# Layers 0 and 1: the first six projection chunks as split products, the narrow columns in two jobs, and buffers moved to equal places modulo 512 bytes

## What is computed

```
h = rmsnorm(x, mix_norm_g)
u = h @ w_in                       # 1024 wide in; columns for four mixers and four gates
y_ret, y_ssd, y_gla, y_ml = mixers(u)
merged = sum_b sigmoid(gate_b) * (y_b @ w_branch_b)
x = x + merged @ w_out
x = x + ffn(rmsnorm(x, ffn_norm_g))      # layer 0: dense; layer 1: experts, top 2 of 8
```

## Time and profile before

| | us |
|---|---|
| median of three executions | 2686.12 |
| the profiled execution | 2694.53 |
| its span | 2692.7 |
| TensorE busy (MATMUL) | 2500.5 (93%) |
| VectorE busy | 1636.8 (61%) |
| ScalarE busy | 1320.3 (49%) |
| GpSimd busy | 407.1 (15%) |
| head of layer 0, chunks 0 to 5 | 27.78 to 115.95 |
| head of layer 1, chunks 0 to 5 | 563.57 to 648.85 |

### The profile page before, as it was taken

One profiled execution on the slowest core, in us unless ns is written; L12 is line 12 of the kernel. 1 busy time (PEld: TensorE's weight loads), 2 busy tenths in 40 slices (PEclk: granted clock), 3 DMA queues, 4 the chain that ended last, 5 costly groups with the idle time before them and its releaser, 6 DMA issues.

```text
span 2692.7 us, 30881 instructions
## 1 busy us (share of the span) xinstructions
PE 2500.5 (93%) x11365; PEld 1986.7 (74%) x11365; DVE 1636.8 (61%) x2327; ACT 1320.3 (49%) x1687; POOL 407.1 (15%) x224
## 2 busy tenths in 40 slices
PE   6999899989998799999999999989998997998998
PEld 5876588878865687777777877868767885776786
DVE  1465655534565598898888988963446544244554
ACT  1343244413332387777777877834534442543443
POOL 2254100003551000000000000024520002551000
PEclk9999899999998899999999999999999998999999
DMA  6433275424241599999999999953456533346550
GB/s 196 142 110 138 99 248 185 139 91 163 94 167 64 173 368 318 322 348 307 322 349 306 331 340 315 343 156 116 151 190 224 188 119 111 135 169 217 188 188 32
DMA packets 373374, 549.30 MB, mean 204 GB/s; under 512 B 20948, under 2 KB 273224, under 8 KB 373144
## 3 DMA queue, kind: packets, MB, share of 16 engines
q1 hardware_dynamic: 369072, 535.82, 58.4%
q0 software_dynamic: 3776, 9.80, 1.3%
q10 hardware_dynamic: 432, 2.37, 0.2%
HBM read 546.91 MB, written 1.05 MB: 203 GB/s over the span
## 4 chain that ended last, share of the span: by engine, by line
PE 65%; DVE 7%; issue 2%; ACT 2%; DMA 2%; POOL 1%; DVEq 0%; SPq 0%; ACTq 0%
PE mb L863 12%; PE mb L865 12%; PE mb L864 12%; PE pb L863 5%; PE pb L865 5%; PE pb L864 5%; PE pb L841 3%; PE pb L1236 2%; PE pb L846 2%; DMA ring<-in_w_in 1%; DVE w_lo L2360 1%; POOL w_lo L719 1%; PE mb L1191 1%; PE pb L932 1%; DVE gates L1911 1%
## 5 line engine op out<-in xcount | busy, mean ns | idle before, releaser
L2360 DVE TENSOR_TENSOR w_lo<-ring,w_hi 128x1024 fp32r<-128x1024 f32 x384 | 461.6, 1223 | 177.8 <-ACT w_hi L1520 128.1
L863 PE MATMUL mb<-w_hi,hT_hi 128*128 128x512 f32 x1232 | 499.0, 405 | 10.6 <-DVE w_lo L2360 6.4
L865 PE MATMUL mb<-w_lo,hT_hi 128*128 128x512 f32 x1232 | 485.1, 394 | 0.0
L719 POOL TENSOR_TENSOR w_lo<-ring,w_hi 128x1024 fp32r<-128x1024 f32 x152 | 370.9, 2464 | 533.3 <-ACT w_hi L1520 533.0
L1520 ACT ACTIVATE w_hi<-ring 128x1024 fp32r<-128x1024 f32 x280 | 285.9, 1054 | 312.2 <-DMA ring<-in_w_in 186.8
L2360 DVE TENSOR_TENSOR w_lo<-down_w,w_hi 128x1024 fp32r<-128x1024 f32 x242 | 295.4, 1223 | 93.3 <-ACT w_hi L1520 79.1
L863 PE MATMUL pb<-w_hi,hT_hi 128*128 128x512 f32 x736 | 300.2, 408 | 10.3 <-DVE low_rows L2360 7.6
L865 PE MATMUL pb<-w_lo,hT_hi 128*128 128x512 f32 x736 | 291.7, 396 | 0.0
L864 PE MATMUL pb<-w_hi,low_rows 128*128 128x512 f32 x736 | 290.9, 395 | 0.0
L1653 ACT ACTIVATE w_hi<-ring 128x1024 fp32r<-128x1024 f32 x256 | 268.1, 1056 | 24.3 <-PE mb L865 18.6
L863 PEld LDWEIGHTS mb<-w_hi,hT_hi 128*128 128x128 f32 x1232 | 232.6, 189 | 62.2 <-DVE w_lo L2360 12.1
(11 more groups left out here) (441 smaller groups left out, 3774.9 us busy)
## 6 DMA issues: line engine op xcount, KB each, us to landing
ring<-in_moe_w SPq DMA_DIRECT2D x128, 1024.0 KB, 7.9
ring<-in_w_in SPq DMA_DIRECT2D x48, 2048.0 KB, 7.9
down_w<-in_moe_w SPq DMA_DIRECT2D x88, 1024.0 KB, 10.6
third_gu<-in_moe_w SPq DMA_DIRECT2D x48, 1024.0 KB, 8.9
down_w<-in_w_ffn_down SPq DMA_DIRECT2D x22, 1024.0 KB, 9.9
ring<-in_w_out SPq DMA_DIRECT2D x8, 2048.0 KB, 8.0
ring<-in_ffn_w SPq DMA_DIRECT2D x16, 1024.0 KB, 8.1
ring<-in_w_ffn_gate SPq DMA_DIRECT2D x16, 1024.0 KB, 5.4
```

What stands on the lines that cost most here:

```text
L719: nc.gpsimd.tensor_tensor(w_lo[:, m % NPIECE], source[m][0], w_hi[:, m % NPIECE].bitcast(F32), ALU.subtract).then_inc(pool_split, 1)
L863: mm(o, a_hi, hi, start=start, stop=False)
L865: return mm(o, a_hi, lo, start=False, stop=stop)
L2360: return tt(dst, src, hi.bitcast(F32), ALU.subtract)
```

## The change

- Chunks 0 to 5 of layers 0 and 1 become split products. `GA` leaves chunk 2, the eight `MI`/`MF` columns leave chunk 4 and the four `SDT` columns leave chunk 5. They have 512 columns each (chunk 4: 256), that is 22 pieces per layer (`HEAD_PIECES`), each with 24 split matmuls of 256 columns. Chunk 2 is loaded by two DMAs of 256 columns.
- The narrow columns are loaded by three small DMAs behind chunk 0, straight to a part of `scratch`, and done as plain fp32 matmuls in two jobs of their own between chunk 0 and chunk 1. The matmuls with `alpha_w` move from behind chunk 5 to behind chunk 1.
- ScalarE rounds the pieces of the head, VectorE takes their low parts. Four pieces are rounded before `hT` is emptied; the high and low parts of `hT` are made bank by bank ahead of chunk 0. VectorE's convolutions are cut into pairs of blocks with low parts between them, and `softplus` is cut in two and moved forward, to the time of chunks 3 and 4. ScalarE's `high_to` calls are spread over the head.
- SP may load a slot again when the low part of its last piece is made.
- ScalarE empties both tokens' halves of a bank with one instruction where before there were two jobs.
- Buffers whose size is an odd multiple of 32 bytes get 32 bytes behind them (`in_lines`), `ea` moves into `small`, and 448 bytes stand between `down_w` and `fhT_hi`.

```diff
+STEP, LINE = 8, 16
 CHUNKS1 = [
-    (SZ, 512, [("ch", ((SX, 128), (SX + 128, 128))), ("tok", 0, SZ, 256), ("tok", 1, SZ, 256)]),
...
-    (SDT, 516, [("ch", ((GQ, 128), (GK, 128))), ("tok2", 0), ("tok2", 1)]),
+    ((SZ, 512), [("toks", SZ, 0), ("ch", SX, 256)]),
+    ((SB, 512), [("ch", SB, 0), ("ch", SC, 256)]),
+    ((GR, 256, MQ, 256), [("toks", GR, 0), ("ch", MQ, 256)]),
+    ((MK, 512), [("ch", MK, 0), ("toks", MV, 256)]),
+    ((MO, 256), [("toks", MO, 0)]),
+    ((GQ, 512), [("ch", GQ, 0), ("toks", GV, 256)]),
...
+NARROW = ((GA, RANK), (SDT, 4), (MI, 8))
...
+        def in_lines(stack, name, shape, dt):
+
+            tensor = stack.enter_context(nc.sbuf_tensor(name, shape, dt))
+            if -(-math.prod(shape[1:]) // STEP) * STEP % LINE:
+                stack.enter_context(nc.sbuf_tensor(name + "_rest", [P, STEP], F32))
+            return tensor
...
+        narrow_w = scratch[:, 256:256 + KD * 28].rearrange("p (k n) -> p k n", k=KD)
-        ea = sb("ea", [P, 2, 4])
+        ea = small[:, 150:158].rearrange("p (l h) -> p l h", l=2)
...
         down_w = sb("down_w", [P, NSLOT, DN_W])
+        sb("down_rest", [P, 112])
...
+                if item[0] == "narrow":
+                    L, at = item[1], 0
+                    if L:
+                        sp.wait_ge(y_ready, 4 * L)
+                    for col, n in NARROW:
+                        sp.dma_start(narrow_w[:, :, at:at + n], a["w_in"][L][:, col:col + n].rearrange("(k p) n -> p k n", p=P)).then_inc(narrow_in, 16)
+                        at += n
+                    continue
...
             def chunk(L, c):
-                lo, n, js = CHUNKS1[c]
-                w = weights((L, "proj", c))
-                for j, spec in enumerate(js):
-                    proj_job(BK[L], ("proj", c, j), w, lo, n, spec)
+                for q in range(count):
+                    m = PC.of[(L, "proj", c, q)]
...
+                    if c == 0:
+                        pe.wait_ge(hT_mix_split, 4 * L + q + 1)
+                    pe.wait_ge(*low_done(m))
...
+                                if kind == "toks":
+                                    it = slice(half * P, (half + 1) * P)
+                                    ins = split_product(bank[:, half * MW:(half + 1) * MW], hT_hi[:, k, it], hT_lo(k)[:, it], m,
+                                                        slice(at, at + MW), first, last)
+                                else:
...
+                                    mm(o, hi, hT_hi[:, k], start=first, stop=False)
+                                    mm(o, lo, hT_hi[:, k], start=False, stop=False)
+                                    ins = mm(o, hi, hT_lo(k), start=False, stop=last)
...
@@ VectorE, mixers(L)
-                acted(B, ("proj", 0, 0))
+                low_range(M0, M0 + 2)
+                hT_low(L, (0, 1))
+                low_range(M0 + 2, M0 + 3)
+                hT_low(L, (2,))
+                low_range(M0 + 3, M0 + 4)
+                hT_low(L, (3,))
...
+                low_range(M0 + 4, M0 + 10)
                 acted(B, ("proj", 1, 1))
...
-                convolve(L, 0, 6, 0, 24)
-                acted(B, ("proj", 3, 0))
-                convolve(L, 6, 4, 30, 46)
-                hT_low(L)
-                acted(B, ("proj", 5, 2))
+                convolve(L, 0, 6, 0, 24, (0, 1))
+                low_range(M0 + 10, M0 + 11)
+                convolve(L, 0, 6, 0, 24, (2, 3))
+                low_range(M0 + 11, M0 + 12)
+                convolve(L, 0, 6, 0, 24, (4, 5))
+                low_range(M0 + 12, M0 + 14)
+                acted(B, ("narrow",))
                 v.wait_ge(alpha_mm, L + 1)
                 softplus(L)
+                low_range(M0 + 14, M0 + 16)
+                softplus_end(L)
+                low_range(M0 + 16, M0 + 19)
+                acted(B, ("proj", 3, 0))
+                convolve(L, 6, 4, 30, 46, (0, 1))
+                low_range(M0 + 19, M0 + 20)
+                convolve(L, 6, 4, 30, 46, (2, 3))
+                low_range(M0 + 20, M0 + 22)
...
@@ ScalarE, before and in mixers(L)
-                turned(BK[L], 0)
+                high_to(MIX[L] + 4)
+                for q in range(4):
+                    turned(BK[L], 0, hT, (q,))
+                    hT_high(L, (q,))
...
+                high_to(M0 + 7)
+                proj(L, 0)
...
+                high_to(M0 + 11)
+                proj(L, 1)
+                high_to(M0 + 15)
+                proj(L, 2)
```

More of the change, by code:

```diff
@@ L10 @@
+import math
 import numpy as np
@@ L167, in bank_jobs1 @@
     jobs = [("turn", k) for k in range(4)]
-    for c, (_, _, js) in enumerate(CHUNKS1):
+    for c, (_, js) in enumerate(CHUNKS1):
         jobs += [("proj", c, j) for j in range(len(js))]
+        if c == 0:
+            jobs += [("ga",), ("narrow",)]
     gate = lambda b, h: [("gate", b, h, i) for i in range(T)]
@@ L196, in split_items1 @@
 def split_items1():
-    items = [("proj", 6), ("proj", 7)]
+    items = [("proj", c) for c in range(len(CHUNKS1))]
     items += [("gate", b, h) for b in range(NBR) for h in range(2)]
@@ L539, in split_item @@
             s = ring_slot()
[L540 to L543 removed]
+            cols = lo if isinstance(lo, tuple) else (lo, 512)
+            width = sum(cols[1::2])
+            count = width * KD // PIECE
+            first = PC.of[(L,) + key + (0,)]
+            loads = []
+            for n, c0 in enumerate(cols[0::2]):
+                at = sum(cols[1:2 * n:2])
+                loads.append((cols_view(width, at), w[:, c0:c0 + cols[2 * n + 1]].rearrange("(k p) n -> p k n", p=P)))
+            add_item((L,) + key, s, loads, low_done(first + count - 1))
+            for q in range(count):
+                source[first + q] = (ring[:, s, q * PIECE:(q + 1) * PIECE], find[(L,) + key] if q == 0 else None)
         def ffn_items(u, L, w1, w3, w2):
@@ new lines, in narrow @@
+            def narrow(L):
+                pe.wait_ge(narrow_in, 48 * (L + 1))
+                for q in range(4):
+                    pe.wait_ge(act_emptied, BK[L].emptied(("turn", q))[1])
+                bank = open_bank(BK[L], ("ga",))
+                for k in range(KD):
+                    ins = mm(bank[0:RANK, 0:S], narrow_w[:, k, 0:RANK], hT[:, k, :], start=k == 0, stop=k == KD - 1)
+                ins.then_inc(filled, 1)
+                bank = open_bank(BK[L], ("narrow",))
+                for i in range(T):
+                    for k in range(KD):
+                        ins = mm(bank[:, 16 * i:16 * i + 12], hT[:, k, i * P:(i + 1) * P], narrow_w[:, k, RANK:], start=k == 0, stop=k == KD - 1)
+                ins.then_inc(filled, 1)
@@ L913, in gate, with alpha @@
+            def alpha(L):
+                acted(BK[L], ("ga",))
+                if L:
+                    pe.wait_ge(gla_put, 5 * L)
+                for i in range(T):
+                    ins = mm(mb[0][:, i * P:(i + 1) * P], ch_in[0:RANK, 12, i * P:(i + 1) * P], alpha_w[:, L, :],
+                             start=True, stop=True)
+                ins.then_inc(alpha_mm, 1)
             def gate(L, b, h, half):
@@ L1395, in _ @@
                     turn(mb[0][:, 0:P], rows, ident).then_inc(rows_turned, 1)
-                for c in range(1, 6):
-                    chunk(L, c)
+                narrow(L)
+                chunk(L, 1)
                 if L == 0:
                     pe.wait_ge(perch_ready, 1)
+                alpha(L)
+                for c in range(2, 6):
+                    chunk(L, c)
                 mixers(L)
@@ L1512, in high_parts, with narrowed @@
+            def narrowed(L):
+                B = BK[L]
+                bank = pb[B.index[("ga",)] % 4]
+                empty(B, ("ga",), (ch_in[0:RANK, 12], bank[0:RANK, 0:S], ACT.Copy, 1.0))
+                both = pb[B.index[("narrow",)] % 4][:, 0:32].rearrange("p (t n) -> p t n", t=T)
+                empty(B, ("narrow",), (u_gla[:, :, 0:4], both[:, :, 0:4], ACT.Copy, 1.0),
+                      (u_ml[:, :, ML_O + MW:], both[:, :, 4:12], ACT.Copy, 1.0))
             def high_parts(lo, hi):
@@ L1875, in norm, with convolve @@
                         op1=ALU.mult).then_inc(xn_ready, 1)
-            def convolve(L, first, count, wcol, bcol):
-                for b in range(count):
+            def convolve(L, first, count, wcol, bcol, blocks):
+                for b in blocks:
                     blk, o = first + b, 50 * L
```

182 lines of the change are left out of this document (94 added, 88 removed).

## The result

| | us |
|---|---|
| before, median of four executions (2684.01 to 2691.84) | 2688.94 |
| after, median of four executions (2663.34 to 2669.47) | 2667.56 |
| ratio, with its 95% interval | 0.9922 (0.9902 to 0.9941) |
| the profiled execution of after | 2668.96 |
| its span | 2667.2 |

The kernel is 21.4 us faster. The forecast was 40 us less, 2646; the time lies in the range of 2630 to 2680. Between the two profiled executions the difference is 25.6 us, because the profiled execution of before was a long one.

The account below looks back on a forecast made before the run. A head lasts as long as its TensorE matmuls. From the profiled 2694.5 us, 16 for the heads and 24 for the buffer places were taken, giving 2654.5; against the median 2686.1 − 40 = 2646, range 2630 to 2680.

Parts of the forecast that it names:

- The price of a product: Heads of layers 0 and 1: a split matmul of 256 columns takes 0.1205 us, between bounds of 0.112 and 0.192.
- The slower rival: Heads: 256 columns don't hide a weight load, 0.192 us a product; 2698 us, without the places' gain 2722; chance 0.09.
- Feeding it: Heads: TensorE waits for VectorE's low parts behind convolutions and softplus, gaps of 10.2 us a layer, a head 81.5 us.
- The starts: Start of chunk 0: layer 1 begins 1.4 us earlier, layer 0 6.0 us later, at 33.8.
- Behind the heads: After the heads: softplus waits (3.8, 3.1 us), slow clock (3.4 a layer) and `xdt` wait (1.1) go; 1.3 a layer lost.
- Heads in all: Layers 0 and 1, heads, starts and what follows: 4.8 and 11.5 us gained, together 16, from 5 to 28.
- The places: Split products of experts and dense down products: realigned operands cut 0.233 to 0.227 us a step, 24 us in all.
- At no cost: Small loads, chunk loads, GpSimd's first piece of chunk 6 and evacuations in layers 0 and 1 stay hidden: 0 us.
- The places not the cause: Dense and expert down products are slow because each goes to another bank, not from buffer places; 2670 us, chance 0.21.
- Experts held by their loads: Experts can't go faster because of their DMA loads, so their 19.5 us are lost; 2665 us, chance 0.07.
- Heads giving nothing: Heads of layers 0 and 1: gaps longer than walked, each brings the clock down; 2662 us, chance 0.07.
- the first rival: Dense layers and experts: the displaced buffers cost nothing, so the 24 us aren't gained; 2670 us, chance 0.21.

Follow-up runs that it names:

- the places alone: Kernel before with only a 480-byte filler ahead of `fhT_hi`, `fhT_lo` and `xg_lo`, putting them on multiples of 512 bytes: 2670.04 us, ratio 0.993.
- The experiments on the order: Changed kernel plus 28 idle transposes, VectorE's head work cut finer and ScalarE's exp before silu: 2655.32 us; then chunk 6's low parts moved from GpSimd to VectorE: 2645.10.
- the kernel with 56 instructions more: Changed kernel plus 28 idle transposes of the identity on TensorE ahead of everything: 2658.49 us, ratio 0.9883.
- the fastest kernel: Changed kernel plus 28 idle transposes, finer VectorE order in the heads, and chunk 6's low parts on VectorE instead of GpSimd: 2645.10 us, ratio 0.9831.

## Why the prediction was right or wrong

The runs give a ladder of medians from a before of 2687.36 us: the places alone −17.3 (2670.04), the heads on top of them −11.6 (2658.49, the kernel with TensorE's packets where before had them), and the place of the packets +9.1 (2667.56 of after, measured beside 2688.94). That is −19.8 against −21.4 measured directly; each of these differences is uncertain by some 4 us.

- **The price of a product.** 0.1205 was forecast, 0.120 measured; the lower bound was the right neighbour. (10.64 less 32 × 0.216 leaves 0.1165 for a record with 4 columns, and not 0.112, since the stretch has the ends of its jobs in it; the starts do lie 0.112 apart.) The narrow jobs took 3.6 and 3.7 us, 3.5 and 3.6 were forecast. The slower rival (0.192) didn't occur.
- **Feeding it.** Gaps of 0.4, 2.4, 2.4, 3.5 and 1.5 us were walked. The starts show three of 1.8, 2.1 and 3.5 beyond the price of a product; the one of 0.4 was not seen in layer 0, and the last was 0.8 in layer 1. From the first product to chunk 6, head 1 took 82.1 us, 81.5 were forecast. Of head 0's 84.1, about 2 are the slow clock of chunk 0's first products. The experiments on the order confirm the cause and show that it wasn't VectorE's total: with the work in another order and four low parts more for VectorE the gaps went from about 7 to 1.1 us.
- **The starts.** Layer 0 at 34.46 where 33.8 was forecast; layer 1 1.3 us earlier against its transposes where 1.4 was forecast.
- **Behind the heads.** The waits for softplus are gone, `xdt` waits 0.4 us. The six steps that took 11.1 us took 2.8, as priced. The low clock in the gap, priced at 1.3 us a layer, came: 3.4 us at 1.2 GHz behind the gap of 3.3.
- **Heads in all.** 16 us forecast; 5.4 + 10.2 = 15.6 by the stages, 11.6 between medians, whose intervals leave room for either. Over more traces it is as much: layers 0 and 1 together take 621.3 us in the mean of the three with the old heads and 606.6 in that of the seven with the new ones in the order of the change. This step held.
- **The places.** The mechanism was right and the term mis-sized: 24 us forecast, 20.6 by the distances over both traces (15 to 17 between medians). The down products came out as priced, 6.7 us in the experts for 7.0 and 5.0 in the dense layers for 4.8. The experts' up products gave 8.9 us for 12.5: I had priced each of three steps at 5.9 ns from one chunk, against a fast distance of 0.227 read elsewhere. Over the whole trace only the step from `hT_hi` to `xg_lo` gained much, 9.7 ns, the two others 1.5 and 3.2, down to 0.228 and 0.229. The fast value has to be read where the same banks and tensors are used, and over many steps.
- **At no cost.** This is the step that failed. For each added operation I named what hides it, and the three small loads, the chunk loads and the evacuations stayed hidden. But I counted only what the instructions do and not that they are there: 712 more of them on TensorE (704 load and product records, 11717 of each where there were 11365, and 8 on semaphores) are no multiple of 256, and from then on the packets of its code met other weight loads than before, eight of the fourteen that layers 2 and 3 wait for and one that the first expert waits for (9.3 us from issue to landing where it had taken 8.0, and a wait for `xg_lo` of 4.9 us where there had been 2.1). The cost, 9 us between medians (15 between the profiled executions of after and of the kernel with 56 instructions more), is half of what was missing; the smaller terms of places and heads are the rest.
- Not all that layers 2 and 3 lost is this. In layer 2 the first plain products after the transposes took 13.8 us where they had taken 11.5, and 13.6 and 13.4 in the kernels of the places alone and of 56 instructions more, whose loads met no packet. That is clock at 1.2 GHz, 2.3 us, whose cause stays open. It goes with the places more than with the packets: these products are slow in six of the seven traces with distances of 0.227 and in none of the five with 0.233; the seventh is that of the fastest kernel.
- **Rivals.** The places not the cause: refuted by the run that moves them alone. Experts held by their loads: refuted by 103.7 us a pass. Heads giving nothing: refuted. My range held because it reached to the first rival, and not for a reason that I had.
- The 16-byte lines of the Trainium skill (SBUF — State Buffer, under Door 1: The DMA port swizzle) would have made the displacement free; the runs decide against taking that rule for the whole of it, since 32, 64 and 128 bytes cost 6 ns and 256 none.

## What to carry to other kernels

Give stationary and moving operands of fp32r products the same address modulo 256 bytes per partition; a filler ahead of three buffers was worth 17 us here, with no change to the program. When an edit changes the number of instructions of the engine that bounds the kernel, look in the trace for packets of the instruction queue inside the loads that somebody waits for, compare stages that the edit doesn't touch, and try a few idle instructions ahead before you judge the edit. Put short blocks between feeding operations and not long ones, and price each block by who runs beside it.

## What was unexpected of the hardware

- A stationary operand that lay 32, 64 or 128 bytes otherwise modulo 256 than the moving one cost some 6 ns in 227. The Trainium skill (TensorE: Matmul & The Clock Gate, Step-by-step: what each phase is for) says that loading the next weights doesn't steal SBUF read bandwidth from the running matmul; these runs show a small cost that depends on the two addresses, without saying where it arises.
- TensorE's code arrives in packets of 16 KB, one for 256 instructions, and one packet makes a load of 2 MB 1.1 us longer (9.1 instead of 7.9). That it takes a DMA engine from the load is inferred from its own record, which is about as long. The Trainium skill (Runtime: NRT & Kernel Launch, Instruction fetch mechanics) gives the same block of 16 KiB and 256 instructions and calls the cost of crossing one mostly hidden. The trace agrees on the block; the cost is hidden from TensorE's own stream and shows in the loads of others.
- `TENSOR_SCALAR` of 256 columns, with a single SBUF tensor as input beside the per-partition factors in `perch`, was held up by GpSimd as the steps with two were: 2.50 us beside it and 0.41 alone. Not every VectorE instruction is: in the same trace two `RECIPROCAL` of 8 columns took 0.19 us beside it, and 0.20 alone. What makes the difference no run shows.
